# Second block of a two-block transformer kernel: the gate tiles as three products of rounded parts, in loads of 256 columns, and a block product moved behind the attention

## The reference, cut to what matters

```
qlat_l, kvlat_l, krope_l, xm_l, z_l, gmla_l, gml_l = jnp.split(h_l @ w_in, splits, axis=-1)
...
y_mla_l = attend(q_l, jnp.concatenate([k_c, k_l], 1), jnp.concatenate([v_c, v_l], 1))
fc = mlstm_features(xm_c, conv_w, conv_b, w_qblk, w_kblk, w_vblk, w_gate, b_gate)
fl = mlstm_features(xm_l, conv_w, conv_b, w_qblk, w_kblk, w_vblk, w_gate, b_gate)
hc, hl = mlstm_bidir(fc[:4], fl[:4])
out_l = merge(y_mla_l, mlstm_readout(hl, z_l, fl[4], ml_norm, ml_skip), gmla_l, gml_l, w_out)
...
def mlstm_readout(h, z, x_c, ml_norm, ml_skip):
    ...
    return jax.nn.sigmoid(z) * (hn + ml_skip * x_c)
def merge(y_mla, y_ml, g_mla, g_ml, w_out):
    return (jax.nn.sigmoid(g_mla) * y_mla + jax.nn.sigmoid(g_ml) * y_ml) @ w_out
```

## Time and profile before

| | us |
|---|---|
| median of 3 runs | 1962.41 |
| lowest and highest | 1956.23, 1962.47 |
| profiled execution, device time | 1960.12 |
| its span in the trace | 1957.2 |
| PE busy | 1748.5 |
| DVE, ACT busy | 804.1, 606.2 |
| mean granted TensorE clock | 0.947 of full speed |

### The profile page before, as it was taken

The page is one execution under the profiler, slowest core; times in us unless marked ns, Lnnn a source line. Parts: engine busy times, 40 slices in busy tenths (PEclk is TensorE's granted clock), DMA queues, the critical chain, the costliest instruction groups (busy, mean ns, idle before and its releaser), DMA issues.

```text
span 1957.2 us, 27219 instructions
## 1 busy us (share of the span) xinstructions
PE 1748.5 (89%) x11670; PEld 1387.5 (71%) x11670; DVE 804.1 (41%) x1271; ACT 606.2 (31%) x873; POOL 141.7 (7%) x86
## 2 busy tenths in 40 slices
PE   7999989999999999899999999999998975666655
PEld 6899878888898899788999998567987321211111
DVE  4345664555535434665566675343446100000001
ACT  3322441443343223440544464542442100000001
POOL 0043100100000144000100020000000000000000
PEclk9999988999999999998999999999999988778778
DMA  5322422687752323334644422402129999999997
GB/s 225 127 97 86 142 96 99 224 335 311 287 199 68 127 87 112 105 130 159 259 173 162 162 108 70 165 8 86 44 89 429 398 428 427 427 428 428 427 428 321
DMA packets 34536, 414.92 MB, mean 212 GB/s; under 512 B 3824, under 2 KB 4080, under 8 KB 4720
## 3 DMA queue, kind: packets, MB, share of 16 engines
q1 hardware_dynamic: 33984, 410.63, 53.3%
q10 hardware_dynamic: 432, 2.56, 0.3%
HBM read 412.13 MB, written 1.05 MB: 211 GB/s over the span
## 4 chain that ended last, share of the span: by engine, by line
PE 72%; DMA 16%; DVE 5%; ACT 4%; another core or an unknown queue 2%; issue 1%; POOL 0%; SPq 0%; DVEq 0%; ACTq 0%
PE ps L212 52%; DMA high<-in_w_e_up_dram 8%; PE ps L743 7%; DMA high<-in_w_e_gate_dram 5%; PE ps L1540 4%; PE ps L1168 3%; DMA high<-in_w_e_down_dram 3%; DVE high L171 2%; PE ps L1140 2%; ACT high L206 2%; PE ps L782 1%; DMA low<-in_late_dram 1%; PE ps L739 1%; PE ps L1557 1%
## 5 line engine op out<-in xcount | busy, mean ns | idle before, releaser
L212 PEld LDWEIGHTS ps<-rarena 128*128 128x128 f32 x3648 | 447.5, 192 | 16.1 <-DVE low L171 7.8
L212 PE MATMUL ps<-rarena 128*128 128x256 f32 (+1 forms) x3648 | 457.6, 287 | 0.0
L206 ACT ACTIVATE high<-ps 128x256 f32<-128x256 f32 (+2 forms) x188 | 90.9, 484 | 528.3 <-PE ps L1540 193.0
L212 PE MATMUL ps<-rarena,rring 128*128 128x256 f32 x1728 | 231.9, 289 | 3.3 <-DVE rring L171 2.8
L212 PEld LDWEIGHTS ps<-rarena,rring 128*128 128x128 f32 x1728 | 215.0, 192 | 8.3 <-DVE rring L171 3.6
L206 ACT ACTIVATE rarena<-ring 128x2048 fp32r<-128x2048 f32 x76 | 140.4, 1848 | 246.8 <-PE ps L212 187.7
L171 DVE TENSOR_TENSOR rarena<-ring,rarena 128x2048 fp32r<-128x2048 f32 x76 | 168.9, 2223 | 107.2 <-ACT rarena L206 105.8
L212 PE MATMUL ps<-high,ring 128*128 128x256 f32 (+1 forms) x864 | 205.9, 390 | 2.8 <-ACT low L206 2.8
L212 PEld LDWEIGHTS ps<-high,ring 128*128 128x128 f32 x864 | 161.5, 190 | 38.5 <-issue 15.9
L171 DVE TENSOR_TENSOR high<-high,ps 128x512 f32<-128x512 f32 x52 | 35.7, 687 | 295.6 <-PE ps L1540 251.3
L1540 PE MATMUL ps<-high,low 128*32 128x512 f32 x560 | 86.5, 748 | 48.1 <-DMA high<-in_w_e_up_dram 29.2
(11 more groups left out here) (205 smaller groups left out, 1762.1 us busy)
## 6 DMA issues: line engine op xcount, KB each, us to landing
ring<-in_w_in_dram SPq DMA_DIRECT2D x56, 1024.0 KB, 4.9
ring<-in_w_ffn_up_dram SPq DMA_DIRECT2D x22, 2048.0 KB, 9.1
high<-in_w_e_down_dram SPq DMA_DIRECT2D x19, 2048.0 KB, 50.3
high<-in_w_e_up_dram SPq DMA_DIRECT2D x18, 2048.0 KB, 49.6
high<-in_w_e_gate_dram SPq DMA_DIRECT2D x17, 2048.0 KB, 47.2
ring<-in_w_mod_dram SPq DMA_DIRECT2D x12, 2048.0 KB, 7.9
ring<-in_w_in_dram SPq DMA_DIRECT2D x10, 2048.0 KB, 7.8
ring<-in_w_e_up_dram SPq DMA_DIRECT2D x9, 2048.0 KB, 49.5
```

What stands on the lines that cost most here:

```text
L206: return self.e.activation(out, x, f, scale=scale, **kw)
L212: ins = self.e.matmul(out, l, r, start=first and i == 0, stop=end and i == n - 1)
```

## The change

- A gate tile is now 24 fp32r products: for each of 8 feature tiles `hx` by the rounded weights, the rest of `hx` by the rounded weights, `hx` by the rest of the weights. `T.hx` is written rounded; its rest is the part that the other input tiles already use (`T.hc[:, 1, 1]`), now computed in one operation from `T.ymla` instead of from `T.hx`.
- The weights come in twelve loads of 256 columns (1 MB); the rounded copy stands in the slot's other half and the rest overwrites the raw weights.
- ACT rounds the weights of tile u + 2 (`rounded2`) ahead of the Tanh of tile u, DVE makes their rest (`low_weights2`) behind its arithmetic for tile u - 1. Tiles 0 and 1 are prepared ahead of the attention.
- The query-key block product stands behind the attention instead of ahead of the key and value products, and so does its eviction; its load comes after the fourth gate load.
- Some small tiles move, the expert loads use the slots in another order (6, 7, 8, ring, 5, ...), and `yT7` is waited for by the fifth expert load.
- The steps of `gates2()` on every engine, `AT_PLAN`, `QK_STEPS`, `CE_PLAN` and `AHEAD` are as before.

```
-            for nm, c0, o in GATES2:
-                columns(f"t{nm}{o}", a["w_in_2"], 8, c0 + o, 512)
+            for u, (nm, i, ld, c0, z) in enumerate(UNITS2):
+                if u == 8:
+                    load("qkblk", (lambda t: t[:, 0:2048], a["qk_blocks"]))
+                if z == 0:
+                    columns(ld, a["w_in_2"], 8, c0, 256)
...
-            order = [5, 6, 7, 8] + ring_[:1] + [3, 4] + [9, 10] + ring_[1:]
+            order = [6, 7, 8] + ring_[:1] + [5, 3, 4] + [9, 10] + ring_[1:]
...
-                        if n == 5:
+                        if n == 4:
                             S.wait_ge("yT7", "gates2.pe")
...
+                PE.wait_ge("hx7", "ln.x7")
+                for u, (nm, i, ld, c0, z) in enumerate(UNITS2):
+                    wl, wh, o = low_weights(ld), high_weights(ld), unit_columns(z)
+                    PE.wait_ge(f"g2u{u}.lo")
+                    b = take("p", f"{nm}{i}.ps", f"{nm}{i}")
+                    prs = [(fr(w_[:, k, o]), fr(h_[:, k, :])) for k in range(8)
+                           for h_, w_ in ((T.hx, wh), (T.hc[:, 1, 1], wh), (T.hx, wl))]
+                    PE.group(b[:, 0:256], prs[0:12], end=False)
+                    yield
+                    PE.group(b[:, 0:256], prs[12:24], first=False).then_inc(*PE(f"{nm}{i}.ps"))
...
+                for u, (nm, i, ld, c0, z) in enumerate(UNITS2):
+                    yield
+                    if u + 2 < len(UNITS2):
+                        rounded2(u + 2)
+                    out(nm, i)
+                    yield
+
+            def rounded2(u):
+                nm, i, ld, c0, z = UNITS2[u]
+                A.wait_ge(ld)
+                o = unit_columns(z)
+                high_part(f"g2u{u}.hi", high_weights(ld)[:, :, o], raw_part(ld)[:, :, o])
...
             def x_low(i):
                 V.wait_ge(f"hx{i}")
-                low_part(T.hc[:, 1, 1, i, :], T.hx[:, i, :], T.hc[:, 1, 0, i, :], f"ln.x{i}")
+                V.stt(fr(T.hc[:, 1, 1, i, :]), T.ymla[:, i, :], mod[:, i, 0:1], T.hc[:, 1, 0, i, :], add, sub).then_inc(
+                    *V(f"ln.x{i}"))
...
+                for u in range(len(UNITS2)):
+                    yield
+                    if u:
+                        out(*UNITS2[u - 1][0:2])
+                    if u + 2 < len(UNITS2):
+                        low_weights2(u + 2)
+                    yield
+                out(*UNITS2[-1][0:2])
+
+            def low_weights2(u):
+                nm, i, ld, c0, z = UNITS2[u]
+                o = unit_columns(z)
+                V.wait_ge(f"g2u{u}.hi")
+                low_part(low_weights(ld)[:, :, o], raw_part(ld)[:, :, o], high_weights(ld)[:, :, o], f"g2u{u}.lo")
```

77 lines of the change are left out of this document (33 added, 44 removed).

## The result

| | before | after |
|---|---|---|
| median, us | 1962.44 | 1979.03 |
| lowest and highest, us | 1956.23, 1966.30 | 1973.21, 1984.57 |
| profiled execution, us | 1960.12 | 1984.57 |
| its span, us | 1957.2 | 1982.8 |

The ratio is 1.0092, with a 95% interval of 1.0062 to 1.0121: 0.9% slower, on the median 0.6 us from the forecast. So the effect is 17 to 24 us, and the profiled execution, 24.5 us above the one of before, lies at the upper end of it. What follows shows that the forecast's total was nearly right although one of its terms, the part ahead of the cells, had the wrong sign.

What follows compares the result with a forecast made beforehand. PE almost alone bounds the kernel up to the expert weights, then mostly loads in a fixed-length tail. Terms -2.1 + 4.1 + 8.2 + 7.0 = +17.2 us on 1962.41 gave 1979.6 us; range 1970 to 1986, held at about 0.8.

Steps and rivals of the forecast that it cites:

- the part ahead of the cells: Attention up to the cells: 3.8 us gained by 18 steps, 1.1 and about 0.6 lost, -2.1 us (bounds -3.8 and 0).
- The three stalls in the cells: PE waits of 6.5 us before round 3's second `ch`, 6.1 before round 5's bank 1 differences, 4.7 before round 7's first `ch`.
- the second term: Cells from round 5's stall on: bank 1's eviction waits behind tile 16's rest; `ch` ends 9.1 us late, net +8.2 us.
- the way to round 5: Cells, first stall: second `ch` starts 5.2 us late, less five gate steps' gain of 0.21 us each: +4.1 us.
- The clock behind them: Behind the three stalls in the cells PE runs at half clock for a time: +7.0 us (bounds 0 and 8.1).
- The term of 0.21: Each gate step (half a tile) takes 1.52 us in the new form instead of 1.73, saving 0.21 us.
- the rounding in ACT's chain to the forget gates: Attention, Tanh behind the forget gates, where PE waited 1.41 us: ACT's rounding adds 1.06 us there.
- The tail: From the first expert load to the refill and on: fixed length, 0 us change, between -1 and +1.
- The block product: 1.9 us of PE leaves the place ahead of the key products and returns behind the attention: 0 in sum.

Runs made afterwards that it cites:

- e3_cells_new: Changed kernel with only gate tiles 9 to 23 in the new form, 0 to 8 as plain f32 products of the rounded hx: 1976.88 us, ratio 1.0085.
- e4_ahead3: Changed kernel, but ACT rounds the weights of tile u + 3 instead of u + 2 at each tile: 1983.65 us, ratio 1.0114.
- e9_rests_half: Changed kernel, but DVE makes the rest of each tile's weights one filler step later: 1981.72 us, ratio 1.0096.
- e10_pool_round: Changed kernel, but POOL instead of ACT rounds the weights from tile 2 on, DVE's rests unmoved: 1951.75 us, ratio 0.9957.
- e8_warm: Changed kernel plus 48, 44 and 36 extra unused PE products where PE stands still in the cells: 1976.87 us, ratio 1.0076.
- e1_allf32: Changed kernel with all 24 gate tiles as plain f32 products, no rounding or rest, the moves kept: 1960.92 us, ratio 1.0002.
- e5_pool: Changed kernel, but POOL instead of DVE makes the weights' rests from tile 2 on, ACT still rounding: 1972.43 us, ratio 1.0055.
- e2_attn_new: Changed kernel with only gate tiles 0 to 8 in the new form, 9 to 23 as plain f32 products: 1965.49 us, ratio 1.0012.
- e12_warm_att: Changed kernel plus 20 extra unused PE products in the attention, ahead of the eighth head's scores: 1973.51 us, ratio 1.0075.
- e6_pool_all: Changed kernel, but POOL both rounds the weights and makes their rests from tile 2 on: 1956.45 us, ratio 0.9965.

## Why the prediction was right, and where it was not

**The three stalls in the cells: shown.** Their places, what ends them and their lengths came as worked out (6.5, 6.1, 4.7 forecast; 6.65, 6.05, 5.21 measured, the third less close than the others). All of it shifted by the 7.1 us that the cells began late: the fourth cell's Exp ended at 1398.5 + 7.1 = 1405.6 in the forecast's working and at 1405.6 in the trace, the second `ch` was to begin at 1402.8 + 7.1 = 1409.9 and began at 1409.98. The working needed only the order on each engine and durations from rows. `e3_cells_new` shows that they need nothing from the attention, `e4_ahead3`, `e9_rests_half` and `e10_pool_round` together that they need the late rounding and not the work: with equal instruction counts on PE and DVE (and in the first two on ACT) the cells went from 97.6 to between 77.6 and 84.6 us.

One sum in the working is off by 1.0 us: from 1428.5 the steps 0.4 + 3.1 + 1.3 + 3.1 + 3.1 end at 1439.5, not at 1440.5. Carried through, the second term would be +7.2 and not +8.2, the total +16.2, the forecast 1978.6. With the clock held (`e8_warm`) the way to round 5 is 3.9 us longer than before and the rest of the cells 8.9 us, against 4.1 and 8.2 forecast, so the slip made this term look better than its working.

**The clock behind them: shown, a little over-sized.** Forecast 7.0 us (bounds 0 and 8.1), measured 5.4 by `e8_warm`. The cells in sum: forecast 4.1 + 8.2 + 7.0 = 19.3, or 18.3 with the sum put right; measured 18.3. The forecast rested on one stall of 6.68 us; here the clock fell behind 6.65, 6.05 and 5.21 us as well.

The Trainium skill (TensorE: Matmul & The Clock Gate, HAM oscillation) tells of waits between stretches of matmul work after which the engine starts cold again. The trace agrees for all three.

**Ahead of the cells: wrong, by its sign.** The step was -2.1 us, with bounds of -3.8 and 0. Against `e1_allf32`, which has all the moves, the attention and what follows took +5.6 us. The parts of this:

- The steps. In `e10_pool_round`, where ACT and DVE add nothing to the waits, the stage is 5.2 us shorter, with 0.3 us more of PE's waits: 18 steps save 5.4 us, 0.30 each. The term of 0.21 was too small. In the cells too: the stage is 1.8 us shorter with 2.8 us more of waits (0.40, 0.70 and 2.58 against 0.92), and the stretch at half clock behind the last of them costs some 1.5 us (the half tile and the 8 records shown above take 4.7 us to the next row, the same pair at full clock 3.1 to 3.2). That is 6.1 us for 22 steps, 0.28 each. The row of the first block missed two things: four steps in a row take 1.42 us each (1376.72 to 1382.40 in this trace), and the row ahead of a single step ends sooner (14 records of 257 columns take 2.84 us to the step instead of 3.03).
- The waits. In the kernel after they sum to 7.1 us (2.88, 1.14, 1.15, 0.21, 0.79, 0.97), in `e1_allf32` to 3.4: +3.7. I had 1.1 for the rounding in ACT's chain to the forget gates; it made 1.5 (1.41 to 2.88). I had missed that of 1.15 us: DVE's scan stands behind the rest of a tile there, which waits for a rounding, the mechanism of the cells in small:

```profile
1339.87 1.23 DVE L171 TENSOR_TENSOR rring<-ring,rring 128x1024 fp32r<-128x1024 f32 x1 [5.22 <-ACT rring L206]
1341.20 0.68 DVE L171 TENSOR_TENSOR low<-ps,low 64x512 f32<-64x512 f32 x1
1341.92 1.22 DVE L2757 TENSOR_TENSOR_SCAN low<-high,low 64x512 f32<-64x512 f32 x1
```

- The clock, 5.6 + 5.4 - 3.7 = 7.3 us by difference. This is what failed: the sum ahead of the cells had no term for the clock. I counted a fall only behind stalls of about 5 us and more, since the one that I had read was of 6.68. `e5_pool` checks the parts: it has 3.3 us more of waits than `e1_allf32`, but only one short stretch, and its attention takes 0.8 us less. So the waits alone do not make the loss, the clock does.

With the clock held, these parts give -1.7 us, near the forecast, but in part because a gain that was too small (3.8 for 5.4) met waits that were too small (1.7 for 3.7); the trace of `e8_warm`, with one stretch, has +0.4.

**The tail: right.** From the end of the cells to the refill 66.1 us against 66.7, forecast 0 within -1 and +1.

**The block product: nearly right in sum, wrong in its parts.** It was to leave and return 1.9 us. Taking it away ahead of the attention shortened that stage by only 0.8 us in every trace; PE then waits 0.78 us for DVE before the first scores, which covers part of it. I had named no cover there. So 1.1 us is left up to the cells. The 0.8 us less behind the cells in `e1_allf32` is within what that stage differs by itself.

**Why the total fits nevertheless.** The sum of the parts is 24 us in the profiled executions, 17.2 in the forecast. Of the first six executions three were at 1982 to 1985 and three at 1973 to 1976, and the median lies between. That the forecast met it within 1 us is luck of some 7 us: the missing clock ahead of the cells is in the traced execution, and the median stands between two groups. That it lay in its range is owed to the cells.

**What stays open.** Why the clock falls at 1307.59 without an idle time, between products of 16 columns and a half tile, is not settled. It does so at this place in both traces of the kernel after and in those of `e2_attn_new`, `e4_ahead3`, `e9_rests_half` and `e12_warm_att`, and not in that of `e8_warm`, which has the same instructions there. `e5_pool`, `e6_pool_all` and `e10_pool_round` have the same products and no such fall, but each is one trace, with an earlier head. So it is open how much of the 7.3 us a wait brings and how much the new products by themselves, and whether the executions of one kernel at 1973 and at 1984 us differ by these stretches.

## What to carry to other kernels

Where a step is split over two engines (one rounds, the other takes the difference), look at each engine's list for what stands behind the waiting instruction: three operations of 1.2 us that waited for roundings of 1.1 us cost up to 20 us in one stage, because ready work of others queued behind them. Give the first half of such a pair to an engine that has nothing to wait for but the load; here both tries to place the halves otherwise in the busy engines' lists relieved the cells and opened stalls elsewhere. And give the clock a term of its own, with a range, wherever waits are added, short ones too.
